# Adaptive modulation by running sums over features, and the first products tile by tile

## The chip, the cores and the metric

The kernel runs on one core of one Trainium2 chip. The metric is device microseconds (us) from start to end of one execution; lower is better. Engines are named as in the profile: PE is TensorE, DVE is VectorE, ACT is ScalarE, SP issues all transfers.

## The reference

Everything is fp32. A first block of 512 tokens by 1024 features is followed by two more layers, which the change does not touch. What matters here is the modulation and the first product:

```python
mod = jax.nn.silu(c) @ w_ada[layer] + b_ada[layer]          # c: 1 x 1024, w_ada: 1024 x 6144
shift1, scale1, gate1, shift2, scale2, gate2 = [
    m[:, None, :] for m in jnp.split(mod, N_MOD, axis=-1)]
h = rms_norm(x, g_pre_mix[layer]) * (1.0 + scale1) + shift1
proj = h @ w_in[layer]                                      # 1024 x 3584
```

`gate1`, `shift2`, `scale2` and `gate2` are needed later: `gate1` after the output projection, `shift2` and `scale2` ahead of the first MLP product, `gate2` after the MLP.

## The kernel before, in words

**Units.** All matrices reach the core in units of 128 x 1024 fp32, 512 KB each, through a ring of five buffers `RAW`. SP issues unit i when the buffer of unit i-5 was consumed (semaphore `s_taken`, raised by DVE). `unit_list` writes the order by hand: the 16 `ada` units of scale1 and shift1 first (j = 1, then j = 0), then the 28 units of `w_in`, one further `ada` unit behind each of 24 of them, then the rest.

**Products in three terms.** A weight unit is split into two parts that PE takes at full rate: ACT rounds it to `WH` (L1603), DVE subtracts to get `WL` (L904, the function `lo_to`). Activations are split the same way, into `HH` (ACT) and `HL` (DVE). Each tile product is three matmuls of 128 x 512 (L443, L444, L445, the function `three`). The first four `w_in` units are the values: one `group` of 96 matmuls, 12 for each of the 8 feature tiles k. Then each `w_in` unit is one `column` of 24 matmuls: 8 of queries and keys (`qk`), 4 of gates (`g`), 12 of the convolution. `walk` lets ACT and DVE prepare units up to two or three columns ahead of PE; there are four slots of `WH` and `WL`.

**Modulation.** In an `ada` unit the 128 partitions are 128 of the 1024 inputs, the free dimension the 1024 features of one of the six vectors. DVE multiplies it by silu(c), one scalar for each partition, and adds it to an accumulator of 128 x 1024 (L853 for the first, L856 for the next seven). After eight units PE adds up the partitions: for the gates with `ONES` as the stationary operand (L407, one row in every partition), for scales and shifts with eight matmuls of one column (L401, 16 rows in the trace), which leave features in partitions in bank 7. DVE adds the bias into `MOD` (L873) and so frees bank 7.

**The start.** Transfers: `VEC` (94 KB), `CST` (97.5 KB, with the identity matrix and the rotary frequencies), `X` in one piece (2048 KB), five `ada` units (2560 KB), positions (256 KB, one row read into all partitions), then units as buffers come free. ACT squares the tokens (L1689); after seven modulation units DVE computes the norm factors (`token_factors`, L1004 and ten small instructions) and both engines scale the tokens (`normed_tokens`, L1693, L1011). PE transposes them in 32 steps (L602); ACT and DVE copy them to `Z`. When scale1 and shift1 are there, ACT writes `HH` (L1805) and DVE `TMP` (L1149) and `HL` (L1156), and the first product starts. The rotary angles are computed by DVE and ACT between these (from L1109). After each `qk` column DVE rotates it (`rotate`, L1172 to L1176, four instructions).

## Time and profile before

| | |
|---|---|
| median of 3 runs | 1545.19 us (1545.18 to 1547.71) |
| profiled execution, its own time | 1542.9 us |
| its span in the profile | 1541.1 us |
| PE busy | 1474.4 us, 96% |
| DVE busy | 880.6 us, 57% |
| ACT busy | 546.9 us, 35% |
| matmuls | 7232 |
| read from memory | 155.65 MB, 102 GB/s over the span |

The profile is one execution, 1542.9 us long; its span, from the first instruction to the last, is 1.8 us shorter. A busy share is the time in which an engine had an instruction in work. Waits are put down to the engine or transfer whose end released them.

### The profile page before, as it was taken

The numbers are of one execution on the slowest core, as the hardware profiler recorded it, in microseconds if no ns is written. First come the engines' busy times: TensorE is split into PE (matmuls) and PEld (weight loads), VectorE is DVE, ScalarE is ACT, GpSimd is POOL, SyncE is SP. The second block draws the span as 40 slices with busy tenths as digits, with TensorE's granted clock in tenths as the row PEclk, the third lists the DMA queues.
The fourth block names the chain that finished last, engine by engine and source line by source line (L and its number), as shares of the span: only waits on it lengthen the run. The fifth ranks groups of instructions, "written<-read, shape, count | busy, mean of one in ns | idle before, by whom it ended". The sixth has DMA issues, their size and how long they took to land.

```text
span 1541.1 us, 18491 instructions
## 1 busy us (share of the span) xinstructions
PE 1474.4 (96%) x7232; PEld 1221.7 (79%) x7232; DVE 880.6 (57%) x1702; ACT 546.9 (35%) x957; POOL 0.2 (0%) x4
## 2 busy tenths in 40 slices
PE   2899999899999999999999899999999999999897
PEld 2778777788888888798888788888888888888776
DVE  5886646554333333665466434524778777787435
ACT  2412123632223223542232323533345434444331
POOL 0000000000000000000000000000000000000000
PEclk9899999999999999999999999999999999999999
DMA  8745322153222223213232222322222111111111
GB/s 303 272 160 206 121 83 96 56 185 143 96 96 96 96 96 110 82 58 121 100 106 83 96 96 82 110 96 77 74 69 69 69 69 69 64 64 67 68 69 55
DMA packets 43526, 158.94 MB, mean 103 GB/s; under 512 B 4784, under 2 KB 5040, under 8 KB 43312
## 3 DMA queue, kind: packets, MB, share of 16 engines
q1 hardware_dynamic: 43440, 157.76, 29.1%
q8 instruction: 58, 0.95, 0.3%
q14 instruction: 28, 0.23, 0.0%
HBM read 155.65 MB, written 2.10 MB: 102 GB/s over the span
## 4 chain that ended last, share of the span: by engine, by line
PE 89%; DVE 5%; ACT 3%; issue 1%; DMA 1%; SPq 0%; ACTq 0%; DVEq 0%
PE PS L443 27%; PE PS L445 26%; PE PS L444 26%; PE PS L728 1%; DMA RAW<-in_ada 1%; PE PS L776 1%; PE PS L739 1%; DVE Z L856 1%; PE PS L780 1%; PE PS L770 1%; PE PS L748 1%; PE PS L756 1%; PE PS L625 1%; PE PS L634 1%; PE PS L804 1%
## 5 line engine op out<-in xcount | busy, mean ns | idle before, releaser
L443 PE MATMUL PS<-HH,WH 128*128 128x512 f32 (+1 forms) x1152 | 459.8, 399 | 4.3 <-ACT TMP L1705 2.3
L445 PE MATMUL PS<-HH,WL 128*128 128x512 f32 (+1 forms) x1152 | 438.0, 380 | 0.0
L444 PE MATMUL PS<-HL,WH 128*128 128x512 f32 (+1 forms) x1152 | 436.6, 379 | 0.0
L904 DVE TENSOR_TENSOR WL<-RAW,WH 128x1024 fp32r<-128x1024 f32 x226 | 274.8, 1219 | 81.5 <-ACT WH L1603 81.3
L1603 ACT ACTIVATE WH<-RAW 128x1024 fp32r<-128x1024 f32 x226 | 238.1, 1056 | 195.7 <-PE PS L445 168.2
L443 PEld LDWEIGHTS PS<-HH,WH 128*128 128x128 f32 x1152 | 218.5, 190 | 46.0 <-issue 6.3
L445 PEld LDWEIGHTS PS<-HH,WL 128*128 128x128 f32 x1152 | 218.3, 189 | 42.0
L444 PEld LDWEIGHTS PS<-HL,WH 128*128 128x128 f32 x1152 | 218.9, 190 | 40.3 <-issue 3.6
L443 PE MATMUL PS<-WH,ZH 128*128 128x512 f32 x400 | 156.7, 392 | 3.9 <-issue 3.9
L444 PE MATMUL PS<-WL,ZH 128*128 128x512 f32 x400 | 156.6, 391 | 0.0
L445 PE MATMUL PS<-WH,ZL 128*128 128x512 f32 x400 | 156.4, 391 | 0.0
L951 DVE TENSOR_TENSOR ZL<-Z,ZH 128x512 fp32r<-128x512 f32 x52 | 35.5, 690 | 144.4 <-ACT ZH L1660 144.4
L443 PE MATMUL PS<-WH,HH 128*128 128x512 f32 x224 | 90.6, 404 | 7.3 <-DVE Z L1390 3.3
L443 PEld LDWEIGHTS PS<-WH,ZH 128*128 128x128 f32 x400 | 75.7, 189 | 20.1 <-issue 4.3
L445 PE MATMUL PS<-WH,HL 128*128 128x512 f32 x224 | 89.0, 397 | 0.0
L1660 ACT ACTIVATE ZH<-Z 128x512 fp32r<-128x512 f32 x52 | 32.2, 629 | 159.7 <-PE PS L445 159.7
L444 PE MATMUL PS<-WL,HH 128*128 128x512 f32 x224 | 88.8, 396 | 0.0
L445 PEld LDWEIGHTS PS<-WH,ZL 128*128 128x128 f32 x400 | 75.7, 189 | 15.9
L444 PEld LDWEIGHTS PS<-WL,ZH 128*128 128x128 f32 x400 | 75.7, 189 | 15.7
L1270 DVE TENSOR_TENSOR Z<-TMP 128x512 f32<-128x512 f32 x32 | 22.0, 692 | 90.7 <-ACT TMP L1870 90.6
L1870 ACT ACTIVATE TMP<-PS 128x512 f32<-128x512 f32 x32 | 19.0, 597 | 110.1 <-PE PS L445 109.9
L443 PEld LDWEIGHTS PS<-WH,HH 128*128 128x128 f32 x224 | 43.1, 193 | 17.7 <-DVE Z L1390 3.7
(223 smaller groups left out, 1666.8 us busy)
## 6 DMA issues: line engine op xcount, KB each, us to landing
RAW<-in_w_fc SPq DMA_DIRECT2D x64, 512.0 KB, 3.2
RAW<-in_hgrn_in SPq DMA_DIRECT2D x64, 512.0 KB, 3.2
RAW<-in_ada SPq DMA_DIRECT2D x48, 512.0 KB, 3.7
RAW<-in_pool_in SPq DMA_DIRECT2D x40, 512.0 KB, 3.2
RAW<-in_w_in SPq DMA_DIRECT2D x28, 512.0 KB, 4.5
RAW<-in_pool_out SPq DMA_DIRECT2D x16, 512.0 KB, 3.2
RAW<-in_hgrn_out SPq DMA_DIRECT2D x16, 512.0 KB, 3.2
RAW<-in_w_out SPq DMA_DIRECT2D x8, 512.0 KB, 3.2
```

The lines of the kernel that those rows point to most:

```text
L443: e.matmul(out, wh, xh, start=first, stop=False)
L444: e.matmul(out, wh, xl, start=False, stop=False)
L445: return e.matmul(out, wl, xh, start=False, stop=last)
L625: e.matmul(PS[b][:, 0:n], Z[:, 12 + h, 128 * i:128 * i + 128], Z[:, 8 + h, 128 * i:T], start=True, stop=True).then_inc(banks.full[b], bank ...
L634: m = e.matmul(PS[ob][:, 128 * i:T], VT[:, i, 128 * h:128 * h + 128], RETA[:, RETO[i]:RETO[i] + n], start=i == 0, stop=i == 3)
L728: m = e.matmul(PAIR[:, 256 * i:256 * i + 192], t.f[:, c], t.qp[:, i, :], start=True, stop=True)
L904: e.tensor_tensor(lo, RAW[:, i % NR, :], hi.bitcast(F32), ALU.subtract).then_inc(taken.sem, taken(i))
L951: e.tensor_tensor(lo, Z[:, k, :], hi.bitcast(F32), ALU.subtract).then_inc(zlo.sem, zlo(z))
L1270: e.tensor_tensor(Z[:, f, :], TMP[:, f % 2, :], TMP[:, f % 2, :], ALU.mult).then_inc(zdone.sem, zdone("fc1", f))
L1603: e.activation(place(s)[0], RAW[:, i % NR, :], ACT.Copy).then_inc(whi.sem, whi(s))
L1660: e.activation(z_place(z)[0], Z[:, k, :], ACT.Copy).then_inc(zhi.sem, zhi(z))
L1870: e.activation(TMP[:, f % 2, :], PS[f if f < 4 else f % 7][:, :], ACT.Relu).then_inc(banks.free[f if f < 4 else f % 7], 1)
```

## The change

`shift1`, `scale1`, `shift2` and `scale2` are computed with the features in the partitions. Their `ada` units are stored transposed: 128 features by the 1024 inputs. DVE multiplies such a unit by a row of silu(c), held in all partitions as `CB`, and the same instruction adds up its products along the free dimension (`accum_out`) into one column of `MOD`. So one unit gives 128 finished values and needs no PE. The gates keep the old way.

The order of units changes with it. The first 20 are four times: one `w_in` unit, then scale and shift of feature tile f, then of tile f+1. The four `w_in` units of the first group thus come between. The token tiles are transposed into banks 4 to 7, the first four ahead of the group and the others after its first four tiles. ACT reads a tile from its bank with scale and shift (new L1791), then rounds it to `HH` (L1794), DVE forms `HL` (`first_low`, new L1130), and PE multiplies tile k as soon as `HL` of tile k is there. Rotary angles now stand ahead of the norm factors on DVE. `c` is loaded as a row into all partitions (512 KB); `CST` is loaded behind the first five units; `X` comes in four pieces; the masks are loaded as bytes (128 KB for 512 KB) and DVE's cast of them goes. Behind `w_in` 12, 13 and 14 stand two `ada` units in place of one.

```diff
 def unit_list():
 
 
-    out = [("ada", 8 * j + k, False) for j in (1, 0) for k in range(8)]
+    out = []
+    for f in range(8):
+        if f % 2 == 0:
+            out.append(("w_in", f // 2, True))
+        out += [("ada", 2 * f, False), ("ada", 2 * f + 1, False)]
     ada = iter(range(16, 48))
-    for n in range(28):
+    for n in range(4, 28):
         out.append(("w_in", n, True))
-        if 1 <= n <= 24:
-            out.append(("ada", next(ada), False))
+        if n <= 24:
+            out += [("ada", next(ada), False) for _ in range(2 if 12 <= n < 15 else 1)]
     for name, n in (("w_out", 8), ("w_fc1", 32), ("w_fc2", 32), ("pool_in", 40), ("pool_out", 16),
                     ("hgrn_in", 64), ("hgrn_out", 16)):
         for i in range(n):
...
-            e.dma_start(CST[:, :], a["cst"][:, 0:C_D]).then_inc(s_cst, 16)
-            e.dma_start(X[:, :, :], a["x"].rearrange("(i p) d -> p i d", p=128)).then_inc(s_x, 16)
+            e.dma_start(flat(0), a["rows"][5].partition_broadcast(128)).then_inc(s_c, 16)
+            e.dma_start(POSI, a["positions"].partition_broadcast(128)).then_inc(s_pos, 16)
+            for t in range(4):
+                e.dma_start(X[:, t, :], a["x"][128 * t:128 * t + 128, :]).then_inc(s_x[t], 16)
             for i in range(NR):
                 load(i)
...
                 j, k = divmod(UNITS[i][1], 8)
-                if k < 7:
+                if j not in (2, 5) or k < 7:
                     return
                 e.wait_ge(taken.sem, taken.of(i))
-                if j in (2, 5):
-                    gate_row(j, 0, 7)
-                    if j == 2:
-                        gate_row(j, 1, 3)
-                    return
-                claim(7)
-                for c in range(8):
-                    m = e.matmul(PS[7][:, 16 + c:17 + c], ACCS[1 if j == 1 else 0][:, 128 * c:128 * c + 128],
-                                 ONES[:, 0:1], start=True, stop=True)
-                m.then_inc(banks.full[7], banks.fill(("ada", j), 7))
+                gate_row(j, 0, 7)
+                if j == 2:
+                    gate_row(j, 1, 3)
...
+            def first_tokens(f):
+                b = 4 + f % 4
+                claim(b)
+                for t in range(4):
+                    m = e.transpose(PS[b][:, 128 * t:128 * t + 128], normal("x", t)[:, 128 * f:128 * f + 128],
+                                    IDN)
+                m.then_inc(banks.full[b], banks.fill(("x", "t", f), b))
+
-            run(group([("v", j) for j in range(4)], [0, 1, 2, 3], True, "in"))
+            e.wait_ge(s_cst, 16)
+            e.wait_ge(normed.sem, normed.of("x", 2))
+            e.wait_ge(own.sem, own.of("normed", "x", 3))
+            for f in range(4):
+                first_tokens(f)
+            for k, _ in enumerate(group([("v", j) for j in range(4)], [0, 1, 2, 3], True, "in")):
+                if k < 4:
+                    first_tokens(4 + k)
...
                 j, k = divmod(UNITS[i][1], 8)
-                src, sc, acc = RAW[:, i % NR, :], COL[:, k:k + 1], ACCS[1 if j == 1 else 0]
+                src = RAW[:, i % NR, :]
                 e.wait_ge(*landed(i))
-                if k == 0:
-                    if j > 1:
-                        e.wait_ge(*banks.made(("ada", 2, 1) if j == 3 else ("ada", j - 1 if j > 2 else 0)))
-                    e.tensor_scalar(acc, src, sc, None, ALU.mult).then_inc(taken.sem, taken(i))
+                if j == 3 and k == 0:
+                    e.wait_ge(*banks.made(("ada", 2, 1)))
+                if j in (3, 4) or k:
+                    e.wait_ge(taken.sem, p.acc)
+                if j in (3, 4):
+                    e.scalar_tensor_tensor(out=ACC, in0=src, scalar=1.0, in1=CB[:, :], op0=ALU.mult,
+                                           op1=ALU.mult, accum_out=MOD[:, 8 * j + k:8 * j + k + 1]).then_inc(
+                                               taken.sem, taken(i))
+                elif k == 0:
+                    e.tensor_scalar(ACC, src, COL[:, k:k + 1], None, ALU.mult).then_inc(taken.sem, taken(i))
                 else:
-                    e.wait_ge(taken.sem, p.acc)
...
 
+            def first_modulation(f):
+
+                for j in (1, 0):
+                    i = UNITS.index(("ada", 2 * f + 1 - j, False))
+                    e.wait_ge(*landed(i))
+                    if f:
+                        e.wait_ge(taken.sem, taken.of(UNITS.index(("ada", 2 * f - 1 - j, False))))
+                    c = 8 if j else 16
+                    e.scalar_tensor_tensor(out=flat(6 if j else 4), in0=RAW[:, i % NR, :], scalar=1.0,
+                                           in1=CB[:, :], op0=ALU.mult, op1=ALU.mult,
+                                           accum_out=MOD[:, c + f:c + f + 1]).then_inc(taken.sem, taken(i))
...
+            e.wait_ge(s_c, 16)
+            e.wait_ge(copied.sem, copied.of("silu row"))
+            e.tensor_tensor(CB[:, :], flat(2), flat(0), ALU.mult).then_inc(own.sem, own("cb"))
+            e.wait_ge(s_pos, 16)
+            e.wait_ge(s_cst, 16)
+            e.tensor_copy(TN, POSI).then_inc(own.sem, own())
...
+                e.scalar_tensor_tensor(out=ANG, in0=TN, scalar=-part, in1=ANG, op0=ALU.mult,
+                                       op1=ALU.add).then_inc(own.sem, own())
+            token_factors("x", 0, 4)
+            normed_tokens("x", 3)
+
+            def first_low(k):
+                e.wait_ge(hhi.sem, hhi.of("in", k))
+                e.tensor_tensor(HL[:, k, :], TMP[:, 2 + k % 2, :], HH[:, k, :].bitcast(F32),
+                                ALU.subtract).then_inc(hlo.sem, hlo("in", k))
+
+            p.next, p.hi, p.unit = 20, 4, 4
+            for f in range(8):
+                if f % 2 == 0:
+                    lo_to(f // 2 + 1)
+                first_modulation(f)
+                if f:
+                    first_low(f - 1)
+                if f == 1:
+                    e.scalar_tensor_tensor(out=TN, in0=ANG, scalar=-1.0, in1=ANG, op0=ALU.mult,
+                                           op1=ALU.max).then_inc(own.sem, own("angle"))
+            first_low(7)
+            lo_to(5)
+            e.wait_ge(copied.sem, copied.of("cos"))
+            e.tensor_tensor(TN, SIN, SIN, ALU.mult).then_inc(own.sem, own())
+            e.scalar_tensor_tensor(out=SIN, in0=SIN, scalar=CST[:, C_SGN:C_SGN + 1], in1=COS,
+                                   op0=ALU.mult, op1=ALU.mult).then_inc(own.sem, own())
+            lo_to(6)
+            e.wait_ge(own.sem, own.n)
+            e.tensor_scalar(COS, TN, -2.0, 1.0, ALU.mult, ALU.add).then_inc(own.sem, own("rot"))
...
+            e.wait_ge(s_c, 16)
+            e.activation(flat(2), flat(0), ACT.Sigmoid).then_inc(copied.sem, copied("silu row"))
...
-            normed_tokens("x", 0)
-            normed_tokens("x", 1)
-            for f in range(0, 8, 2):
+            for t in range(3):
+                normed_tokens("x", t)
+            e.wait_ge(own.sem, own.of("gb"))
+            for f in range(8):
+                b = 4 + f % 4
+                if f % 2 == 0:
+                    hi_to(f // 2 + 1)
+                e.wait_ge(taken.sem, taken.of(UNITS.index(("ada", 2 * f, False))))
+                e.activation(GA[:, f:f + 1], MOD[:, 8 + f:9 + f], ACT.Identity,
+                             scale=VEC[:, V_GPRE1 + f:V_GPRE1 + f + 1], bias=GB[:, f:f + 1]).then_inc(
+                                 copied.sem, copied())
+                e.wait_ge(taken.sem, taken.of(UNITS.index(("ada", 2 * f + 1, False))))
+                e.activation(MOD[:, f:f + 1], MOD[:, 16 + f:17 + f], ACT.Identity,
+                             bias=VEC[:, V_BADA + f:V_BADA + f + 1]).then_inc(copied.sem, copied())
+                if f > 1:
+                    e.wait_ge(hlo.sem, hlo.of("in", f - 2))
                 e.wait_ge(*banks.made(("x", "t", f)))
...
+                e.wait_ge(copied.sem, copied.n)
+                e.activation(TMP[:, 2 + f % 2, :], PS[b][:, :], ACT.Identity, scale=GA[:, f:f + 1],
+                             bias=MOD[:, f:f + 1]).then_inc(banks.free[b], 1)
+                e.wait_ge(*banks.taken(("x", "t", f)))
+                e.activation(HH[:, f, :], TMP[:, 2 + f % 2, :], ACT.Copy).then_inc(hhi.sem, hhi("in", f))
+                if f == 2:
+                    e.wait_ge(own.sem, own.of("angle"))
+                    e.activation(SIN, ANG, ACT.Sin, scale=0.5)
+                    e.activation(COS, TN, ACT.Sin, scale=-0.5, bias=CST[:, C_HPI:C_HPI + 1]).then_inc(
+                        copied.sem, copied("cos"))
+            hi_to(6)
```

How the order of instructions moves, at two places. On DVE ahead of the first product, before (units 0 and 1 are scale1's; `s_raw` is a landed unit, `s_square` the last square of ACT):

```order
L1090 TENSOR_TENSOR COL<-COL,VEC 128x8 [waits s_copied]
L853 TENSOR_SCALAR Z<-RAW,COL 128x1024 [waits s_raw0,s_dve]
L856 SCALAR_TENSOR_TENSOR Z<-RAW,COL,Z 128x1024 [waits s_taken,s_raw1]
...
L856 SCALAR_TENSOR_TENSOR Z<-RAW,COL,Z 128x1024 [waits s_taken,s_raw1]
L1004 TENSOR_SCALAR NW<-SSA 128x4 [waits s_square]
```

and now, at the same place (`s_cst` is the landing of `CST`):

```order
L1110 TENSOR_TENSOR CB<-Z 128x1024 [waits s_copied,s_c]
L1113 CAST TMP<-Z 128x512 [waits s_cst,s_pos]
L1115 TENSOR_SCALAR Z<-TMP,CST 128x512 [waits s_dve]
L1117 TENSOR_SCALAR TMP<-Z 128x512 [waits s_dve]
L1120 TENSOR_SCALAR TMP<-TMP 128x512 [waits s_dve]
L1123 SCALAR_TENSOR_TENSOR Z<-TMP,Z 128x512 [waits s_dve] x4
L1023 TENSOR_SCALAR NW<-SSA 128x4 [waits s_square]
```

The norm factors stood behind seven modulation units and now stand behind the angles, which wait for `CST`. On DVE in the first group now, feature tiles 4 and 5 (L923 is `WL`, L879 a running sum, L1130 `HL`):

```order
L923 TENSOR_TENSOR WL<-RAW,WH 128x1024 [waits s_whi]
L879 SCALAR_TENSOR_TENSOR Z,MOD<-RAW,CB 128x1024 [waits s_taken,s_raw1]
L879 SCALAR_TENSOR_TENSOR Z,MOD<-RAW,CB 128x1024 [waits s_taken,s_raw2]
L1130 TENSOR_TENSOR HL<-TMP,HH 128x512 [waits s_hhi]
L879 SCALAR_TENSOR_TENSOR Z,MOD<-RAW,CB 128x1024 [waits s_taken,s_raw3]
L879 SCALAR_TENSOR_TENSOR Z,MOD<-RAW,CB 128x1024 [waits s_taken,s_raw4]
L1130 TENSOR_TENSOR HL<-TMP,HH 128x512 [waits s_hhi]
```

and on ACT from the same pair of tiles on (L1781 and L1785 give scale and shift of one tile, L1594 is `WH`):

```order
L1594 ACTIVATE WH<-RAW 128x1024 [waits s_raw0]
L1781 ACTIVATE COL<-MOD,COL,VEC 128x1 [waits s_taken]
L1785 ACTIVATE MOD<-MOD,VEC 128x1 [waits s_taken]
L1791 ACTIVATE TMP<-PS,MOD,COL 128x512 [waits s_copied,s_full4,s_hlo]
L1794 ACTIVATE HH<-TMP 128x512 [waits s_free4]
L1781 ACTIVATE COL<-MOD,COL,VEC 128x1 [waits s_taken]
L1785 ACTIVATE MOD<-MOD,VEC 128x1 [waits s_taken]
L1791 ACTIVATE TMP<-PS,MOD,COL 128x512 [waits s_copied,s_full5,s_hlo]
L1794 ACTIVATE HH<-TMP 128x512 [waits s_free5]
L1594 ACTIVATE WH<-RAW 128x1024 [waits s_raw0]
```

Before, the 16 running sums were done ahead of this group; now DVE's next `WL` waits for ACT's `WH`, which stands behind `HH` of an odd tile, which waits for that tile's sums on DVE.

## Rows read from the trace of the kernel before

**Rows 1.** The page, busy time, share of the span and instructions of each engine.

```profile
PE 1474.4 (96%) x7232; PEld 1221.7 (79%) x7232; DVE 880.6 (57%) x1702; ACT 546.9 (35%) x957; POOL 0.2 (0%) x4
```

**Rows 2.** Timeline, the start: start us, length us, engine, line, operation; in brackets idle, releaser.

```profile
11.10 0.75 DVE L853 TENSOR_SCALAR Z<-RAW,COL 128x1024 f32<-128x1024 f32 x1 [7.99 <-DMA RAW<-in_ada]
...
18.60 2.67 DVE L856 SCALAR_TENSOR_TENSOR Z<-RAW,COL,Z 128x1024 f32<-128x1024 f32 x2 [0.85 <-DMA RAW<-in_ada]
...
21.19 0.16 DVE L1004 TENSOR_SCALAR NW<-SSA 128x4 f32<-128x4 f32 x1
...
22.96 2.19 ACT L1693 ACTIVATE Z<-X,COL 128x1024 f32<-128x1024 f32 x2 [8.54 <-DVE COL L997]
```

**Rows 3.** Transfers: instruction, count, size, median us from issue to landing.

```profile
RAW<-in_w_fc SPq DMA_DIRECT2D x64, 512.0 KB, 3.2
...
G<-in_rows SPq DMA_DIRECT2D x1, 512.0 KB, 4.6
```

**Rows 4.** Timeline, DVE before and in the first group, among them the angles.

```profile
37.26 4.05 DVE L856 SCALAR_TENSOR_TENSOR Z<-RAW,COL,Z 128x1024 f32<-128x1024 f32 x3
...
41.23 0.42 DVE L1109 CAST TMP<-Z 128x512 f32<-128x512 int32 x1
...
44.46 1.22 DVE L904 TENSOR_TENSOR WL<-RAW,WH 128x1024 fp32r<-128x1024 f32 x1
...
59.15 1.41 DVE L1121 SCALAR_TENSOR_TENSOR Z<-TMP,Z 128x512 f32<-128x512 f32 x2
```

**Rows 5.** Page, ACT, costliest groups: rounding a weight unit, reading a bank.

```profile
L1603 ACT ACTIVATE WH<-RAW 128x1024 fp32r<-128x1024 f32 x226 | 238.1, 1056 | 195.7 <-PE PS L445 168.2
...
L1870 ACT ACTIVATE TMP<-PS 128x512 f32<-128x512 f32 x32 | 19.0, 597 | 110.1 <-PE PS L445 109.9
```

**Rows 6.** Timeline, ACT in the first group: sine table and cosine.

```profile
58.14 1.28 ACT L1792 ACT_TABLE_LOAD   x1
...
63.52 0.73 ACT L1795 ACTIVATE Z<-TMP,CST 128x512 f32<-128x512 f32 x1 [2.30 <-DVE TMP L1125]
```

**Rows 7.** Timeline, PE: the first product and the first column.

```profile
47.50 0.76 PE L443 MATMUL PS<-WH,HH 128*128 128x512 f32 x1 [2.56 <-issue]
...
50.57 0.40 PE L444 MATMUL PS<-WL,HH 128*128 128x512 f32 x1
...
70.75 0.39 PE L443 MATMUL PS<-HH,WH 128*128 128x512 f32 x1
```

**Rows 8.** Timeline, PE after a pause ahead of the first MLP product.

```profile
285.72 0.36 PE L443 MATMUL PS<-HH,WH 128*128 128x256 f32 x1 [2.35 <-ACT TMP L1705]
```

**Rows 9.** Windows, that stretch: PE, PEld, DVE, ACT, POOL busy, clock, transfer share, GB/s.

```profile
286.00:291.00 5.00, 5.00 (x30) 4.91 (x29) 3.54 (x7) 4.91 (x12) 0.00 (x0) 0.66 0.32 108
```

**Rows 10.** Timeline, PE: gate row, sums over partitions, and the norm sums of the retention.

```profile
85.91 1.98 PE L407 MATMUL PS<-Z,ONES 128*128 128x512 f32 x4 [1.39 <-DVE Z L856]
...
131.32 1.95 PE L401 MATMUL PS<-ONES,Z 128*128 128x1 f32 x16
...
193.03 1.84 PE L401 MATMUL PS<-ONES,Z 128*128 128x1 f32 x16
...
211.31 1.02 PE L580 MATMUL PS<-ONES,TMP 128*128 128x1 f32 x8 [1.64 <-DVE MOD L873]
```

**Rows 11.** Timeline, DVE in the columns of queries and keys.

```profile
96.11 0.69 DVE L1172 TENSOR_TENSOR TMP<-PS,Z 64x512 f32<-64x512 f32 x1 [0.82 <-PE PS L445]
...
98.85 1.28 DVE L856 SCALAR_TENSOR_TENSOR Z<-RAW,COL,Z 128x1024 f32<-128x1024 f32 x1
100.05 1.22 DVE L904 TENSOR_TENSOR WL<-RAW,WH 128x1024 fp32r<-128x1024 f32 x1
101.56 0.69 DVE L1172 TENSOR_TENSOR TMP<-PS,Z 64x512 f32<-64x512 f32 x1 [0.29 <-PE PS L445]
...
105.49 0.68 DVE L882 TENSOR_TENSOR G<-PS,Z 128x512 f32<-128x512 f32 x1
...
108.14 1.22 DVE L904 TENSOR_TENSOR WL<-RAW,WH 128x1024 fp32r<-128x1024 f32 x1
```

More of the change, by code:

```diff
@@ L209, in build @@
             pass
+        with nc.sbuf_tensor("CB", [128, 1024], F32) as CB:
+            pass
         QP = [sb(f"QP{i}", [128, 4, 192]) for i in range(2)]
@@ L1079, in diagonal @@
                 p.spread = name
-            def gains(dst, j, g, one):
-                e.wait_ge(*banks.taken(("ada", j)))
-                e.scalar_tensor_tensor(out=COL[:, dst:dst + 8], in0=MOD[:, 8 * j:8 * j + 8],
-                                       scalar=1.0 if one else 0.0, in1=VEC[:, g:g + 8], op0=ALU.add,
-                                       op1=ALU.mult).then_inc(own.sem, own())
             e.memset(ONES[:, :], 1.0).then_inc(own.sem, own("ones"))
+            e.wait_ge(s_vec, 16)
@@ L1160, in vector_program @@
-            run(group(), turns)
-            run(turns)
-            e.wait_ge(s_msk, 16)
-            e.tensor_copy(MSK[:, :], flat(14)).then_inc(own.sem, own("masks"))
+            e.scalar_tensor_tensor(out=GB, in0=VEC[:, V_BADA + 8:V_BADA + 16], scalar=1.0,
+                                   in1=VEC[:, V_GPRE1:V_GPRE1 + 8], op0=ALU.add, op1=ALU.mult).then_inc(
+                                       own.sem, own("gb"))
+            e.wait_ge(s_c, 16)
+            e.wait_ge(copied.sem, copied.of("silu row"))
@@ L1799, in scalar_program @@
-            turns = angles()
-            next(turns)
-            walk(1)
-            e.wait_ge(*banks.taken(("ada", 0)))
-            for k in range(8):
-                e.wait_ge(*banks.taken(("x", "t", k)))
-                e.activation(HH[:, k, :], Z[:, k, :], ACT.Identity, scale=GA[:, k:k + 1],
-                             bias=MOD[:, k:k + 1]).then_inc(hhi.sem, hhi("in", k))
-                if k in (1, 4):
-                    walk(1 + k // 4)
+            for t in range(3):
+                normed_tokens("x", t)
@@ L1813, in values @@
                 e.activation(VT[:, j, :], PS[j][:, :], ACT.Copy).then_inc(banks.free[j], 1)
-            run(group(values), turns)
-            run(turns)
+            for j in range(4):
+                values(j)
             nb = 0
```

148 lines of the change are left out of this document (36 added, 112 removed).

## The prediction

> **What bounds the kernel now.** First the page: PE is busy for 96% of the span, DVE and ACT are far from it [rows 1]. So only three things can move the time: work that PE no longer does, a wait of PE that goes or comes, and the start, in which PE has nothing to multiply. Then the timeline of the start. The first product begins at 47.50 us and the first column at 70.75 us [rows 7]. Seven matmuls up to 50.57 us run at the low clock level, one in 0.44 us; the other 89 of the group take 20.2 us, 0.227 us each, without a pause. Up to 47.5 us DVE sets the pace with its 16 modulation units, 1.35 us each where one waits for the last [rows 4]. The change attacks this start, so what counts is when the first column can begin. Last, the columns: 5.45 us each (24 by 0.227), in which DVE rotates for 2.74 us and spends 1.20 us on a modulation unit and about 1.2 us on a `WL`, so it has next to nothing in reserve there [rows 11].
>
> **The change, part one: until the group can start.** The norm factors now wait for the angles on DVE, and these for `CST`. Ahead of and with `CST` stand 94 + 512 + 256 + 2048 + 2560 + 97.5 = 5567.5 KB. That is exactly what stood up to the sixth `ada` unit before, which landed at 18.6 us; the first, behind 2751.5 KB, had landed at 11.1 us, so 376 KB/us flow [rows 2]. New among the bytes is the row of `c`, read into all partitions. Such a load took 4.6 us from issue to landing where others of 512 KB took 3.2 us [rows 3]. I add 0.5 us, between nothing and 1.4 us: `CST` lands at 19.1 us. By the section on queues, rings and completion order of the Trainium skill, "DMA: Bandwidth & Descriptors", each engine consumes its descriptors in ring order but completions need not come in the order of issue; if that let the small `CST` pass the units ahead of it, the second rival below would hold. The angles: cast to second product of the range reduction 3.23 us (41.23 to 44.46), two more products 1.41 us [rows 4], so DVE is free at 23.75 us. Factors 1.77 us (21.19 to 22.96) to 25.5 us; ACT scales three tiles, 1.5 times 2.19 us, to 28.8 us [rows 2], and rounds the first `w_in` unit, 1.06 us [rows 5]: at **29.9 us** DVE starts the first `WL`. All five units landed by then, and DVE will be slower (below) than five units in 6.8 us at the rate above, so transfers hide.
>
> **Part two: the group, paced by DVE and ACT in turn.** A running sum reads two fp32 inputs as the old instruction, 1.20 us in sequence [rows 11], and adds up as well. The trace has no such instruction on DVE. If the read of the sum overlaps, it is free; the smallest instructions of DVE take 0.16 us [rows 2], and a full one behind a drained pipe could cost a few tenths. I take 0.1 us, nearest to the small instruction with overlap: 1.30 us, with 0 and 0.3 us as ends. The Trainium skill, "VectorE: DVE Perf Modes", section "Two Vector instructions with no wait between them", says that an op that writes its accumulator is two instructions; it gives no time, and by it the free end would be excluded. Two tiles cost DVE one `WL` 1.2, four sums 5.2 and one `HL` 0.6 us, 7.0 together; the other `HL` fits into what follows. Then DVE waits: ACT needs 0.2 us for the shift, 0.6 us for the bank and 0.6 us for `HH`, 0.2 us of handing over, and 1.05 us for `WH` [rows 5], 2.65 us in all. So a pair takes 9.65 us. The first pair lacks an `HL`: 9.05 us. In the second ACT also does the table load (1.28) and two sines (0.73 each) [rows 6]; counted from the end of the sums of tile 2 at 3.8 us, 1.6 + 2.75 + 0.4 + 1.3 + 1.05 us follow: 10.9 us. The third takes 9.65 us. In the fourth `HL` of tile 6 is ready at 7.6 us. Sum: 9.05 + 10.9 + 9.65 + 7.6 = 37.2 us. PE needs 2.7 us for each of the last two tiles at full clock, which gives 42.6 us. Tile 4 ends near 30.7 us on this scale and `HL` of tile 5 is ready at 34.0 us, so PE pauses for 3.3 us. After a pause of 2.35 us elsewhere PE ran at a granted mean of 0.66 for 5 us [rows 8, 9], thus for 3.4 us at 1.2 GHz, losing 1.7 us of work. Tile 6 follows tile 5 after a pause of 0.5 us that absorbs part, and the low level may begin inside the pause: I add 0.9 us. The column starts at 29.9 + 43.5 = **73.4 us, 2.65 us later than before**. Behind it DVE has about 8.5 us of its own work (three `WL`, three sums, three rotary steps) and 15 us until the third column needs it: hidden.
>
> **Part three: PE's sums over partitions.** Ahead of the group they stood beside DVE's work and are worth nothing by themselves. In the columns two sets of L401 go, 1.95 and 1.84 us [rows 10], with PE otherwise busy on both sides: **3.7 us less**. DVE's bias addition into `MOD` held bank 7, and PE waited for it 1.64 us ahead of the retention's norm sums [rows 10]. This wait goes; PE's next matmuls are columns for which DVE had reserve: **1.6 us less**, with 0 as the other end, should DVE be late there anyway.
>
> **Part four: two modulation units in one column.** From the end of the `qk` column whose sums close gate1, DVE owes by the `WL` of the third gate column: three rotations 8.2, six sums 8.4, the gate row's four instructions 2.65 (105.49 to 108.14), three `WL` 3.6 us, 22.9 us. PE runs four columns meanwhile, 21.8 us [rows 11]. **1.1 us more**, as a wait of PE ahead of that column; 0 to 2.5 us with the price of a sum. Before, the same place held three units fewer.
>
> **At no cost.** The gate row itself, 1.39 us of waiting and 2 us of matmuls, moves three columns back unchanged [rows 10]. The masks' cast and 384 KB go, both hidden beside PE's columns. The silu row, `CB` and `GB` are done while `CST` is in flight.
>
> **Sum.** +2.65 − 3.7 − 1.6 + 1.1 = −1.55 us. The profiled execution took 1542.9 us, so its like would take 1541.35 us; the median is 2.3 us above it, and I move the median by the same: **1543.6 us**. A difference of 0.2%, 3.1 us, is about what a measurement here tells from none.
>
> **The rivals.**
> - *The sum comes free* (chance 0.27). A running sum takes 1.20 us, as its two inputs alone do [rows 11]. 16 in the group give 1.6 us and six in part four 0.6 us; with the clock kept in the pause 0.9 us more: −4.65 us, 1540.5 us.
> - *`CST` passes the units* (0.05). It lands near 12 us and the angles end before the squares. The start moves up by 5 to 6 us, until running sums wait for their units: some 1538 us. Against it: the flow in order of issue [rows 2].
> - *The running sum is dear* (0.17). This is the case of the other sign. At 0.4 us above my price, 22 sums on the path cost 8.8 us: −1.55 + 8.8 = +7.2 us, 1552.4 us. It decides the sign at 0.07 us above my price, and a slowdown beyond 0.2% from 0.21 us, a running sum of 1.51 us.
> - *The clock falls in each pause and bank 7 gives nothing* (0.08). If the level falls at tile 5 and stays low into tile 6, the group ends up to 2.2 us later; without the 1.6 us: +2.25 us, 1547.4 us. The Trainium skill, "TensorE: Matmul & The Clock Gate", section on oscillation, tells of bursts shorter than the waits between them that start slow each time. Here the trace agrees after its pause [rows 8, 9]; early tiles have time to spare in any case, only the last three count.
>
> **The numbers.** The forecast has 0.43; its own range, with 0.05 us either way on a sum and 0.8 us on the clock, is 1541.5 to 1546.5 us. Faster by over 0.2% (under 1542.1 us) are the first two rivals: 0.32. Slower by over 0.2% (over 1548.3 us) is the third, with some of the fourth and of what I have not seen: 0.20. The rest, 0.48, is within. The range that leaves out two in ten is 1539.5 to 1549.5 us.
>
> **What would show it.** The first `WL` of the changed kernel near 29.9 us, the cast of the angles near 19 us. Running sums of 1.30 us in sequence. DVE idle for ACT's `WH` three times, 2 to 3.5 us. First product near 37 us, first column near 73.4 us, the low clock once late in the group. No L401, no wait ahead of the retention's sums, about 1 us ahead of the third gate column. I am wrong if the cast comes much sooner, or if a running sum is off by 0.1 us, or if PE stands still in the columns for longer than here.

## The result, and the profile after

The changed kernel took 1538.51 us (median of 4 runs, 1536.32 to 1539.49), the kernel before 1546.45 us (median of 4 beside it, 1545.18 to 1548.03): ratio 0.9946, 95% interval 0.9929 to 0.9963, or 7.9 us less. Copies of both, run later, gave 1538.24 us (5 runs) and 1544.41 us (11 runs), the ratio of the changed one 0.9959 (0.9946 to 0.9973), 6.3 us less. The forecast was 1543.6 us; its range ended at 1539.5 us, about 1 us above the result. The profiled execution took 1538.69 us with a span of 1536.9 us, 4.2 us less than the profiled span of before.

The page of the changed kernel, engines' busy time, share and instructions; PE lost 64 instructions, two sets of 16 in the columns and two ahead of the group:

```profile
PE 1467.9 (96%) x7168; PEld 1212.9 (79%) x7168; DVE 874.4 (57%) x1719; ACT 557.2 (36%) x979; POOL 0.2 (0%) x4
```

Timeline of DVE in the changed kernel: start us, length us, engine, line, operation, and in brackets idle time and releaser.

```profile
19.78 0.43 DVE L1113 CAST TMP<-Z 128x512 f32<-128x512 int32 x1 [11.27 <-DMA CST<-in_cst]
...
30.45 1.23 DVE L923 TENSOR_TENSOR WL<-RAW,WH 128x1024 fp32r<-128x1024 f32 x1 [3.45 <-ACT WH L1594]
31.60 1.22 DVE L879 SCALAR_TENSOR_TENSOR Z<-RAW,CB 128x1024 f32<-128x1024 f32 x1
32.74 0.08 DVE L879 DVE_READ_ACCUMULATOR Z<-RAW,CB 128x1 f32 x1
32.74 1.22 DVE L879 SCALAR_TENSOR_TENSOR Z<-RAW,CB 128x1024 f32<-128x1024 f32 x1
33.89 0.08 DVE L879 DVE_READ_ACCUMULATOR Z<-RAW,CB 128x1 f32 x1
...
39.10 1.23 DVE L923 TENSOR_TENSOR WL<-RAW,WH 128x1024 fp32r<-128x1024 f32 x1 [1.64 <-ACT WH L1594]
...
50.06 1.23 DVE L923 TENSOR_TENSOR WL<-RAW,WH 128x1024 fp32r<-128x1024 f32 x1 [3.95 <-ACT WH L1594]
...
59.34 1.22 DVE L923 TENSOR_TENSOR WL<-RAW,WH 128x1024 fp32r<-128x1024 f32 x1 [2.26 <-ACT WH L1594]
```

The first `WL` starts at 30.45 us, 0.55 us behind the forecast, because the cast, which waits for `CST`, starts at 19.78 us and not at 19.1 us. The starts of two running sums, 31.60 and 32.74 us, lie 1.14 us apart (1.145 us on average over two steps), not 1.30 us. The read of the accumulator is a row of its own of 0.08 us, and it starts at the same moment as the next sum: it costs nothing in sequence. The four starts of `WL` are the beats of the group: 8.65, 10.96 and 9.28 us between them, where the prediction had 9.05, 10.9 and 9.65 us.

Timeline of ACT in the changed kernel, the turn of tile 0, and `WH` at the end of tile 1:

```profile
32.86 0.39 ACT L1781 ACTIVATE COL<-MOD,COL,VEC 128x1 f32<-128x1 f32 x1 [2.44 <-DVE Z L879]
34.00 0.29 ACT L1785 ACTIVATE MOD<-MOD,VEC 128x1 f32<-128x1 f32 x1 [0.76 <-DVE Z L879]
34.39 0.78 ACT L1791 ACTIVATE TMP<-PS,MOD,COL 128x512 f32<-128x512 f32 x1
35.20 0.63 ACT L1794 ACTIVATE HH<-TMP 128x512 fp32r<-128x512 f32 x1
...
38.03 1.04 ACT L1594 ACTIVATE WH<-RAW 128x1024 fp32r<-128x1024 f32 x1
```

The prediction had 0.2 us for the shift and 0.6 us for the bank; the rows say 0.29 (0.39 from start to start) and 0.78 us. These small steps stand on the path in each turn too and took back part of what the sums gave.

Timeline of PE in the changed kernel, which answers to [rows 7, 8, 10]:

```profile
37.01 0.76 PE L445 MATMUL PS<-WH,HH 128*128 128x512 f32 x1 [3.87 <-DVE HL L1130]
54.24 0.79 PE L445 MATMUL PS<-WH,HH 128*128 128x512 f32 x1 [4.31 <-DVE HL L1130]
63.51 0.50 PE L445 MATMUL PS<-WH,HH 128*128 128x512 f32 x1 [0.37 <-DVE HL L1130]
...
72.03 0.39 PE L445 MATMUL PS<-HH,WH 128*128 128x512 f32 x1
...
103.50 1.98 PE L409 MATMUL PS<-Z,ONES 128*128 128x512 f32 x4 [1.39 <-DVE Z L863]
130.16 0.50 PE L445 MATMUL PS<-HH,WH 128*128 128x512 f32 x1 [0.18 <-DVE WL L923]
207.50 0.95 PE L582 MATMUL PS<-ONES,TMP 128*128 128x1 f32 x8
```

A window of the group (busy time and count of PE, PEld, DVE, ACT, POOL, then granted clock, transfer share, GB/s):

```profile
54.00:60.00 6.00, 5.76 (x15) 4.50 (x16) 3.74 (x7) 4.34 (x7) 0.00 (x0) 0.50 0.97 321
```

PE pauses for 4.31 us ahead of tile 3 (54.24 us) and runs at the low level behind it, so tiles 3 and 4 take so long that ahead of tile 5 (63.51 us) it pauses for only 0.37 us.

The first column starts 1.28 us later than in [rows 7], not 2.65 us. The gate row waits its 1.39 us as before. Ahead of the third gate column PE waits 0.18 us, not 1.1 us. The sums over partitions are gone, and ahead of the retention's norm sums (207.50 us, against 211.31 us in [rows 10]) there is no wait. At that row the kernel is 3.81 us ahead, and that is nearly all of the 4.2 us that the two spans differ by; the rest arises near 880 us (numbers 1 and 2).

### The profile page after: what moved, and what is told of

It is laid out like the page before. It is cut to its first block, busy times and chain, and to the rows that moved or that the text cites. A ratio compares the mean times of both kernels' runs of the same rounds, so it can differ in the third digit from the quotient of the medians.

```text
span 1536.9 us, 18402 instructions
## 1 busy us (share of the span) xinstructions
PE 1467.9 (96%) x7168; PEld 1212.9 (79%) x7168; DVE 874.4 (57%) x1719; ACT 557.2 (36%) x979; POOL 0.2 (0%) x4
## 4 chain that ended last, share of the span: by engine, by line
PE 86%; DVE 6%; ACT 4%; issue 2%; DMA 1%; SPq 0%; ACTq 0%; DVEq 0%
PE PS L445 26%; PE PS L447 26%; PE PS L446 26%; PE PS L729 1%; PE PS L777 1%; PE PS L740 1%; DMA CST<-in_cst 1%; ACT WH L1594 1%; PE PS L781 1%; PE PS L771 1%; DVE WL L923 1%; PE PS L749 1%; PE PS L757 1%; DVE Z L879 1%; PE PS L626 1%
## 5 line engine op out<-in xcount | busy, mean ns | idle before, releaser
L923 DVE TENSOR_TENSOR WL<-RAW,WH 128x1024 fp32r<-128x1024 f32 x226 | 275.0, 1219 | 92.5 <-ACT WH L1594 92.2
L1594 ACT ACTIVATE WH<-RAW 128x1024 fp32r<-128x1024 f32 x226 | 238.1, 1056 | 195.2 <-PE PS L447 145.0
L1863 ACT ACTIVATE TMP<-PS 128x512 f32<-128x512 f32 x32 | 19.1, 600 | 110.1 <-PE PS L447 109.8
```

The lines of the kernel that those rows point to most:

```text
L923: e.tensor_tensor(lo, RAW[:, i % NR, :], hi.bitcast(F32), ALU.subtract).then_inc(taken.sem, taken(i))
L1594: e.activation(place(s)[0], RAW[:, i % NR, :], ACT.Copy).then_inc(whi.sem, whi(s))
L1863: e.activation(TMP[:, f % 2, :], PS[f if f < 4 else f % 7][:, :], ACT.Relu).then_inc(banks.free[f if f < 4 else f % 7], 1)
```

## The experiments

Each kernel ran beside the kernel before on one chip; the runs of before had medians of 1544.9 to 1545.0 us in all three sets. Unless said otherwise, an edit is made to the changed kernel, whose copy (the same kernel, run again) took 1538.24 us.

**1, 2. The two kernels again.** No edit.

Expected of the copy of before: 

> The kernel before once more, timed against itself, with a second profile. The profiled execution of before (1542.9 us) lies 2.3 to 5.1 us under its four timed ones, while the changed kernel's profiled one (1538.69 us) lies among its own. Theory A, the two profiles differ by 4.2 us and that is the true effect; the rest of the measured 8 us is scatter of before: this run's times spread from 1543 to 1548 us, and so does the ratio. Theory B, before really takes 1546 us and its profile was a lucky execution: all times lie at 1545 us and above, and the new profile shows some 3 us more of low clock or of waiting somewhere.

Expected of the copy of the changed kernel: 

> The changed kernel once more, to have it on the same chip as the others and with five rounds. By theory A (scatter of before) 4 to 5 us below before; by theory B 7 to 8 us below it. The profile shows the first column at 72 us and running sums of 1.15 us again.

Measured: 1544.41 us (1542.56 to 1548.14, 11 runs) and 1538.24 us (1537.05 to 1539.31, 5 runs). So the execution of before on which the sum was built, 1542.9 us, lies at the low end of that kernel's executions, while that of the changed kernel (1538.69 us) lies in the middle of its own. The times of before scatter as theory A had it, and the difference of 6.2 us lies between the 4 to 5 us of A and the 7 to 8 us of B: neither is decided. In the copy of the changed kernel the first column starts at 71.07 us, and its cast comes at 18.80 us in place of 19.78 us. Each run also gives its mean granted clock: on average 0.9861 over 15 runs of before and 0.9894 over the 5 of the copy. The two profiled executions had 0.987 both.

One difference that no edit touches shows in all four profiles. PE pauses for 3.9 us in each, and resumes at 878.88 us in the copy of before and at 873.83 us in the copy of the changed kernel. Windows of 10 us from there on, in this order:

```profile
878.88:888.88 10.00, 10.00 (x34) 8.04 (x35) 4.60 (x6) 2.71 (x4) 0.00 (x0) 0.75 0.35 107
```

```profile
873.83:883.83 10.00, 10.00 (x37) 8.09 (x38) 5.20 (x6) 2.72 (x4) 0.00 (x0) 0.83 0.32 105
```

The low level around this resumption lasts 6.8 us in both profiles of before and 3.4 us in both of the changed kernel (by windows of 0.5 us), and from the resumption to the next transposes by L439 (L441 now), at 966.57 and 960.85 us, the copies take 87.7 and 87.0 us. So the longer low stretch costs 0.6 to 0.7 us. It does not mark the kernel before: of the profiles below, those of numbers 3, 5, 7, 9, 10 and 12 have the long stretch and those of 4, 6, 8 and 11 the short one. What decides between the two stays open.

**3. `CST` ahead of the units.**

```
             e.dma_start(VEC[:, :], a["vec"]).then_inc(s_vec, 16)
+            e.dma_start(CST[:, :], a["cst"][:, 0:C_D]).then_inc(s_cst, 16)
...
             for i in range(NR):
                 load(i)
-            e.dma_start(CST[:, :], a["cst"][:, 0:C_D]).then_inc(s_cst, 16)
```

Expected: 

> One part is changed: CST is loaded right behind VEC in place of behind five units. Theory C, the start is set by the landing of CST: angles then run ahead of the squares, the norm factors start at the end of the squares near 14.3 us in place of 24.5 us, the first WL near 20.5 us in place of 30.45 us, and the kernel gets 9 to 10 us faster than the changed kernel. Rival: units of the matrix then arrive too late for DVE, it waits for RAW in the group, and the gain is 4 us or less.

Measured: 1528.74 us (ratio to before 0.9896, 0.9882 to 0.9909), 9.5 us less than the copy of the changed kernel. DVE of this kernel:

```profile
7.99 0.43 DVE L1113 CAST TMP<-Z 128x512 f32<-128x512 int32 x1 [0.44 <-DMA Z<-in_positions]
...
20.23 1.23 DVE L923 TENSOR_TENSOR WL<-RAW,WH 128x1024 fp32r<-128x1024 f32 x1 [3.45 <-ACT WH L1594]
```

The first `WL` starts 10.22 us earlier than in the changed kernel, and the end moves with it: the theory held. So the wait for `CST` is the start's bound, as part one had it, and no transfer of a unit takes its place.

**4. ACT rounds a weight unit ahead of the odd tile.**

```
                 if f % 2 == 0:
                     hi_to(f // 2 + 1)
+                elif f < 7:
+                    hi_to(f // 2 + 2)
```

Expected: 

> One part is changed: ACT rounds the next w_in unit ahead of the odd tile of a pair in place of behind it. Theory D, DVE's three waits for WH (1.6, 4.0 and 2.3 us) are pauses of the whole group: the group ends 7 us earlier. Rival: the pauses hide another limit, the transfers (five units need 6.8 us, DVE's work for two tiles 7.0 us) or PE at the low clock, and the gain is 4 us or less.

Measured: 1532.85 us (0.9922, 0.9909 to 0.9934), 5.4 us less, between the theory's 7 us and the rival's 4 us. The timeline of DVE shows the four `WL` at 30.31, 37.24, 46.18 and 53.11 us; the second and the fourth wait for nothing, the third 1.93 us. A pair without a wait takes 6.93 us: one `WL`, four sums and two `HL`. The first column starts at 66.71 us, 5.3 us earlier. This shows the alternation of part two: ACT's rounding stood in the turn, and a pair was DVE's work plus that of ACT. Some of the rival is there too, for in the last pair DVE waits 0.84 us for a transfer, which it never does in the changed kernel's group:

```profile
59.20 1.23 DVE L879 SCALAR_TENSOR_TENSOR Z<-RAW,CB 128x1024 f32<-128x1024 f32 x1 [0.84 <-DMA RAW<-in_ada]
```

**5. Eight more products in the group.**

```
                     c = 8 if j else 16
+                    if j:
+                        e.tensor_tensor(ACC, RAW[:, i % NR, :], CB[:, :], ALU.mult)
                     e.scalar_tensor_tensor(out=flat(6 if j else 4), ...
```

The products are read by nobody. Expected: 

> A measurement of how much of a running sum lies on the path of the group: each of the eight tiles gets one more product of two fp32 inputs on VectorE (unit times row, into ACC), ahead of its first running sum, that nobody reads. Theory: DVE and ACT take turns and every sum of the group delays ACT, so all eight count in full: 8 x 1.2 = 9.6 us above the changed kernel. Rival: ACT sets the pace, and DVE, which stands idle for some 9 us in all for ACT's roundings, takes the work in those gaps: 2 to 4 us above it, with those idle times shorter by as much.

Measured: 1547.64 us (1544.44 to 1549.81, 10 runs), 9.4 us more; expected 9.6 us. The first column starts at 80.07 us instead of 72.03 us, 8.0 us later. DVE's idle time ahead of each `WL` is hardly changed: 1.64, 2.81 and 2.26 us, and only the second is shorter, by 1.14 us. From first `WL` (30.33 us) to first column the trace has 8.2 us more. The products take 1.14 us each in sequence, 9.1 us in all, so 0.9 us of them is missing, which is about that shorter wait. The theory held; that 9.4 us came so near to 9.6 us is partly chance, as the trace shows 8.2 us in the group. So an instruction of DVE in the group counts nearly in full (where ACT does not have the sines to do), and the price of a running sum multiplies by 14 to 16.

**6. The factor 1.0 from SBUF.**

```
-                    e.scalar_tensor_tensor(..., in0=RAW[:, i % NR, :], scalar=1.0,
+                    e.scalar_tensor_tensor(..., in0=RAW[:, i % NR, :], scalar=ONES[:, 0:1].bitcast(F32),
```

The same in the columns' running sums. Expected: 

> The running sums take their factor 1.0 from a column of ones in SBUF in place of a constant in the instruction; all 32 of them. The old products with a column as factor took 1.20 us in sequence, the running sums 1.15 us. Theory: the operand in SBUF is what costs the 0.05 us, so the running sums take 1.20 us in sequence and the group ends 16 x 0.05 = 0.8 us later, 1 us in all. Rival: the difference comes from the old form's second operand, which DVE itself had just written, and the running sums stay at 1.15 us: no difference.

Measured: 1540.05 us (1538.57 to 1542.82, 9 runs), 1.8 us more than the copy, and 0.9976 of before (0.9966 to 0.9985). The intervals of the two kernels overlap, but the trace is plain. DVE of this kernel:

```profile
30.64 1.28 DVE L879 SCALAR_TENSOR_TENSOR Z<-RAW,ONES,CB 128x1024 f32<-128x1024 f32 x1
31.84 0.08 DVE L879 DVE_READ_ACCUMULATOR Z<-RAW,ONES,CB 128x1 f32 x1
31.84 1.28 DVE L879 SCALAR_TENSOR_TENSOR Z<-RAW,ONES,CB 128x1024 f32<-128x1024 f32 x1
```

1.28 us each and 1.20 us in sequence: exactly the old instruction of [rows 11]. The theory held: the operand from SBUF costs 0.06 us of an instruction's duration, and adding up costs nothing. From first `WL` (29.49 us) to first column (71.90 us) the group takes 42.41 us against 41.58 us, 0.83 us or 16 x 0.05.

**7. Part three undone.** The group keeps its running sums; scale2 and shift2 are summed by PE:

```
-                if j in (3, 4):
-                    e.scalar_tensor_tensor(out=ACC, in0=src, scalar=1.0, in1=CB[:, :], op0=ALU.mult,
-                                           op1=ALU.mult, accum_out=MOD[...])
...
+                claim(7)
+                for c in range(8):
+                    m = e.matmul(PS[7][:, 16 + c:17 + c], ACC[:, 128 * c:128 * c + 128],
+                                 ONES[:, 0:1], start=True, stop=True)
```

Expected: 

> Only the group's modulation keeps the running sums; scale2 and shift2 are again products on VectorE that TensorE adds up over the partitions (two sets of eight one-column matmuls in bank 7). Theory, as in the prediction's part three: 3.7 us for the two sets and 1.6 us for the wait ahead of the retention's norm sums come back, so 5.3 us above the changed kernel. Rival: the wait for bank 7 gives nothing, 3.7 us above it, and the trace shows DVE late at another place, or PE waiting in the retention by as much as the sums would have saved.

Measured: 1553.5 us (1550.85 to 1556.44, 5 runs), 15.3 us more, three times what both theories gave. The timeline of PE shows where:

```profile
135.87 3.58 PE L410 MATMUL PS<-ONES,Z 128*128 128x1 f32 x16 [3.69 <-DVE Z L866]
...
202.07 1.84 PE L410 MATMUL PS<-ONES,Z 128*128 128x1 f32 x16
...
220.35 1.02 PE L589 MATMUL PS<-ONES,TMP 128*128 128x1 f32 x8 [1.64 <-DVE MOD L895]
```

PE waits 3.69 us for DVE and the sums behind the wait run at the low level, 3.58 us in place of 1.9 us. That level lasts 10.2 us (by windows of 0.5 us from 135 us on), which costs PE an estimated 4.7 us. The wait for bank 7 is there again, at 1.64 us as before. From first column to the last norm sums the trace has 13.6 us more than the changed kernel's (71.24 to 220.35 us against 72.03 to 207.50 us): 3.7 us for the two sets, 5.3 us for the two waits, 4.7 us for the low level. That DVE was late there through the doubled units was the guess. This raised the question of the doubled units, for the next two.

**8. Part four undone.** One modulation unit behind each `w_in` unit up to the 28th:

```
-        if n <= 24:
-            out += [("ada", next(ada), False) for _ in range(2 if 12 <= n < 15 else 1)]
+        out.append(("ada", next(ada), False))
```

Expected: 

> Part four alone is undone: one modulation unit behind each w_in unit up to the 28th, none doubled. By the trace of the changed kernel PE waits only 0.18 us ahead of the third gate column, so the theory is that the doubled units cost next to nothing: 0.2 us less than the changed kernel, which these runs can't tell from none, and that wait is gone from the trace. Rival, the prediction's part four: 1.1 us less.

Measured: 1537.39 us (1535.71 to 1539.56, 5 runs), 0.85 us less, which these runs can't tell from none; the wait of 0.18 us is gone from the trace.

**9. Parts three and four undone** (both edits). Expected: 

> scale2 and shift2 summed by TensorE again, and one modulation unit per column. With the doubled units this undoing cost 15.3 us in place of the 5.3 us of the prediction's part three. Theory: the doubled units put DVE 4 us behind, TensorE asks for the sums in the order of the units and waits for that backlog, twice, and drops to the low clock after it; with one unit per column there is no backlog, the two sets cost their own 3.7 us and the wait for bank 7 1.6 us: 5.3 us above e_single, some 1543.5 us. Rival: the backlog comes from the later start of the columns' modulation in all (four units behind, not three), so it stays: 10 us or more above e_single.

Measured: 1550.09 us (1548.06 to 1551.73, 5 runs), 12.7 us above number 8. So the doubled units explain only 2.6 of the 10 us that were too many in number 7. The theory fell. The rival had the size, but not the place: PE does not wait for DVE at the first set. The timeline of PE:

```profile
152.34 1.84 PE L409 MATMUL PS<-ONES,Z 128*128 128x1 f32 x16
...
160.37 1.83 PE L588 MATMUL PS<-ONES,TMP 128*128 128x1 f32 x8 [3.11 <-DVE MOD L894]
162.07 0.77 PE L451 MATMUL PS<-HH,WH 128*128 128x512 f32 x1
162.64 0.63 PE L452 MATMUL PS<-HL,WH 128*128 128x512 f32 x1
...
222.15 1.95 PE L409 MATMUL PS<-ONES,Z 128*128 128x1 f32 x16 [0.30 <-DVE Z L865]
```

and its windows around both places (clock third from the right):

```profile
158.00:170.00 12.00, 9.63 (x29) 7.26 (x30) 5.07 (x9) 0.41 (x1) 0.00 (x0) 0.72 0.00 1
216.00:230.00 14.00, 13.70 (x60) 10.73 (x59) 8.25 (x21) 2.61 (x4) 0.00 (x0) 0.88 0.44 150
```

In number 8 the clock is 1.00 in both windows. Here PE waits 3.11 us for the addition of the bias, which DVE's program reaches only at 160.07 us, behind the retention's own steps, and then runs at the low level. From these norm sums to the next the trace has 20.3 us, where number 8 has 17.0 us: the low level behind the wait costs 3.3 us more, on top of the wait. Behind the second set it lasts 3.4 us, an estimated 1.7 us of work. Together, 3.8 us for the sets, 3.4 us for the two waits and 5.0 us for the low level are 12.2 us. By the row at which PE waits for `DG` (242.58 us, against 231.01 us in number 8) the trace has fallen back by 12.3 us, counted from the first column (71.24 and 71.96 us); the medians differ by 12.7 us.

**10. Numbers 3 and 4 together.** Expected: 

> CST is loaded right behind VEC, and ACT rounds the next w_in unit ahead of the odd tile; nothing else differs from the changed kernel. Theory: the two act in different places, the one moves the whole group up, the other takes ACT's rounding out of the turn between DVE and ACT, so the gains found for each alone add: 9.5 + 5.4 = 14.9 us less than the changed kernel, some 1523.5 us. Rival 1: with both, DVE asks for five units in less than the 6.8 us that the transfers take for them and waits for landings; then the gain of the second shrinks to about 2 us, 1527 us, and the trace shows waits of DVE for RAW out of the DMA queue in the group. Rival 2: PE pauses more often at the faster pace and loses clock, 1525 to 1527 us, with no wait of DVE for transfers.

Measured: 1522.16 us (0.9862, 0.9848 to 0.9875), 16.1 us less than the changed kernel where the parts add to 14.9 us; the medians do not tell the two apart. The theory held. Windows of the group in this kernel, and in the changed one over the stretch that answers to it:

```profile
20.00:60.00 40.00, 34.53 (x146) 27.67 (x145) 36.40 (x54) 27.55 (x46) 0.00 (x0) 1.00 0.87 308
```

```profile
30.00:70.00 40.00, 31.41 (x120) 24.80 (x119) 30.13 (x47) 24.00 (x41) 0.00 (x0) 0.83 0.77 262
```

DVE is busy for 36.4 of 40 us and waits for no landing in the group. PE still pauses for 3.63 us ahead of its first product and later for 1.12 and 0.71 us, but the clock stays at its high level. Both rivals were wrong.

**11. The first unit rounded ahead of the tokens**, on top of number 10:

```
+            hi_to(1)
             for t in range(3):
                 normed_tokens("x", t)
```

Expected: 

> e_both, and ACT rounds the first w_in unit ahead of scaling the first three token tiles, not behind them. In e_both DVE waits 3.45 us for that rounding. Theory: DVE starts its first WL about 3.3 us sooner and keeps that lead down the group, since every later turn is set by DVE's sums; only ACT's scaled tokens come 1 us later, which the transposes can stand: 2.5 to 3.3 us less than e_both, 1519.3 us. Rival: ACT sets the next turns, as it takes up tile 0 only after its tokens and three transposes, and DVE's lead turns into a wait for the second WH: 0 to 1 us less.

Measured: 1517.68 us (1517.64 to 1520.56, 5 runs), 0.9832 of before (0.9818 to 0.9846): the fastest here, 4.5 us below number 10. The wait of 3.45 us ahead of the first `WL` is 0.34 us; the first column starts at 52.50 us against 55.49 us. Those 3 us are shown. A further 0.7 us comes from the pause of numbers 1 and 2, behind which number 10 has the long low stretch and number 11 the short one; the last 0.8 us lie within what the medians leave open.

**12. The sines behind tile 6**, on top of number 11:

```
-                if f == 2:
+                if f == 6:
                     e.wait_ge(own.sem, own.of("angle"))
                     e.activation(SIN, ANG, ACT.Sin, scale=0.5)
```

Expected: 

> e_first, and the two sines and their table load move from behind tile 2 to behind tile 6. In e_both DVE waits 1.92 us for the WH behind the sines. Theory: that wait shrinks by the 2.7 us that the sines hold ACT, so it goes; behind tile 6 ACT has tile 7 and two roundings ahead of it and the sines put these back by 2.7 us, which the last WL can't stand fully: 0 to 1.9 us less than e_first. Rival: the group's end is set by HL of tile 7, which ACT now reaches 2.7 us later, so it is 1 us or more slower than e_first.

Measured: 1521.73 us (1520.23 to 1522.91, 4 runs), 4.0 us more. The rival had the sign, but not the place. DVE:

```profile
38.91 1.23 DVE L923 TENSOR_TENSOR WL<-RAW,WH 128x1024 fp32r<-128x1024 f32 x1 [1.05 <-ACT WH L1594]
...
48.93 0.69 DVE L1130 TENSOR_TENSOR HL<-TMP,HH 128x512 fp32r<-128x512 f32 x1 [3.00 <-ACT HH L1797]
...
62.91 1.29 DVE L863 SCALAR_TENSOR_TENSOR Z<-RAW,COL,Z 128x1024 f32<-128x1024 f32 x1 [1.81 <-DMA RAW<-in_ada]
```

`HL` of tile 7 waits 3.00 us (1.31 us in number 11), and the first column begins at 52.57 us, no later. But DVE is 0.8 us later at its last `WL` of the group and frees its buffers that much later, the transfers into them are issued 0.8 us later, and at 62.91 us it waits 1.81 us for a landing (0.44 us in number 11), 1.4 us behind number 11. PE pays at the gate row, waiting 2.35 us for DVE instead of 1.39 us.

That is 1.0 us of the 3.3 us by which the two profiled executions differ. The rest lies in stretches that the edit does not touch. PE waits for ACT ahead of transposes at 277.05 us (275.99 us in number 11). Windows behind it, in number 12 and then in number 11:

```profile
277.00:283.00 6.00, 5.95 (x38) 5.98 (x39) 1.95 (x5) 5.03 (x13) 0.00 (x0) 0.72 0.00 0
```

```profile
276.00:282.00 6.00, 6.00 (x52) 6.00 (x53) 2.21 (x6) 5.34 (x14) 0.00 (x0) 1.00 0.00 0
```

From there to the next transposes by that line, at 621.54 and 618.86 us, number 12 takes 1.6 us longer. Near 856 us it has the long low stretch, 0.7 us. So the move is shown to cost 1.0 us in the columns. Whether the two low stretches follow from it or vary from run to run stays open.

## Why the prediction was wrong

The mechanism held in all four parts: the start waits for `CST`, DVE and ACT take turns, the sums of PE and the wait go, and PE waits ahead of the third gate column. What failed are three sizes: the price of a running sum, the place and cost of the low clock in the group, and the step from the profiled execution to the median.

**Part one held.** The cast came at 19.8 us, where the landing of `CST` was forecast for 19.1 us; the first `WL` stood 0.55 us behind the forecast. In the copy the cast came at 18.80 us, so the landing itself scatters by 1 us from run to run.

**Part two failed at the price of the running sum**: "I take 0.1 us, nearest to the small instruction with overlap: 1.30 us". It measured 1.15 us, below even the free end of 1.20 us, because the constant factor saves what the accumulation was feared to cost (number 6). Number 5 shows that such an error counts nearly in full. Two of the 16 sums stand beside ACT's sines and count for nothing, so this term alone was 14 x 0.155 = 2.2 us too high in the group.

The 0.9 us for the clock failed by its place. The prediction had a pause of 3.3 us ahead of tile 5 with the low level behind it. The trace has the pause of 4.31 us ahead of tile 3, with the low level there. Tiles 3 and 4 had time to spare for it, and PE paused for 0.37 us ahead of tile 5. The last three tiles ran from 63.51 to 72.03 us in 8.5 us, against 36 x 0.227 = 8.2 us at full clock.

Against it went the 0.55 us of the start, ACT's steps in three turns, 0.27, 0.43 and 0.30 us too low (from the last sum to `WH`; the bank and the shift too low, the sines too high), and the 0.3 us of the last three tiles. Small differences of `WL` and `HL` take back 0.1 us. Together, −2.2 − 0.9 + 0.55 + 1.0 + 0.3 − 0.1 = −1.35 us; the column came 1.37 us before the forecast.

The clause "by it the free end would be excluded" went wrong with it. The Trainium skill's "VectorE: DVE Perf Modes", section "Two Vector instructions with no wait between them", is right that there are two instructions, and the trace agrees: it has the second row. But that row of 0.08 us lies under the next sum, so two instructions are not two costs here.

**Part three held in size.** 3.8 us for the two sets and 1.64 us for the wait were gone. Numbers 7 and 9 show more: in the new order of units the same PE sums would have cost 12.7 to 15.3 us, since the additions and products that they wait for sit later in DVE's program and the low clock comes with the waits (5.0 us of it in number 9). Taking one part back measures it in its new surroundings, not the share that it had in the change.

**Part four failed by the same price, and by a slip.** 1.1 us was forecast, 0.18 us measured. The prediction put the six sums at 8.4 us, 1.40 us each, where its own price of 1.30 us gives 7.8 us; that alone would have made 0.5 us of the 1.1 us. In the trace of DVE the six take 7.25 us, 1.21 us each, since the second of two in a row starts 1.34 us after the first. Number 8 agrees with the small wait.

**The sum, mended.** −1.55 − 1.37 − 0.92 = −3.84 us, and the trace is 3.81 us ahead at the retention's norm sums. This is "the sum comes free", the first rival, to which the prediction gave 0.27: its price and nearly its size (−4.65 us), though it too moved the result to 1540.5 us only.

**The anchor failed too**, the step from the profiled execution to the median: "the median is 2.3 us above it, and I move the median by the same". Even with −3.84 us this gives 1541.4 us, and 1538.5 us was measured. The medians of before lie 1.5 to 3.6 us above its profiled execution (1544.4 to 1546.5 us against 1542.9 us), those of the changed kernel 0.2 and 0.5 us below its own. So of the 5.1 us between forecast and result 2.3 us are errors of the sum, 2.5 us the anchor, and the remaining 0.3 us arise behind the norm sums, mostly by the shorter low stretch near 880 us.

Why a usual execution of before takes longer than its profiled one stays open. The mean clocks of the runs, 0.9861 and 0.9894, point to more of the low level in before, but a mean clock is not a time. The changed kernel's profile has 41.8 us at the low level in all and its copy 31.8 us, yet the two differ by 1.1 us, of which 1.0 us is there at the first column already, from the earlier cast. 6.8 of these 10 us lay at the first tiles of the group, which have time to spare. Of the kept profiles of before, the copy has 3.4 us more of the low level, at its start (0.69 over 30:52 us in place of 0.77), and its first column comes 0.3 us later.

## What to carry to other kernels

Where two engines take turns, first find out which instructions stand in the turn: there an error of 0.1 us in the price of one is multiplied by their number, and a bound from both sides must also ask what else differs in the instruction, such as where its scalar comes from. What helped far more than the change was to take something out of the turn: a small transfer loaded first (9.5 us) and a rounding done one tile sooner (5.4 us). And a wait of an engine late in one place is priced together with all that is ordered behind it: the same sums over partitions were worth 5.4 us in one order of units and 12.7 to 15.3 us in another.

## What the runs showed that was not expected

- A sum with accumulator over 128x1024 fp32 takes 1.22 us (1.15 us in sequence) with a constant factor and 1.28 us (1.20 us in sequence) with a factor in SBUF; the read of the accumulator, 0.08 us, overlaps the next instruction.
- The low clock after a wait costs more than the wait's row shows: in number 9, behind 3.11 us of waiting and eight matmuls of one column (1.83 us at the low level, 0.95 us else), a window of 12 us had a mean clock of 0.72, and the stretch took 3.3 us longer on top of the wait. In number 10 PE paused up to 3.6 us in the group and the clock stayed at 1.00.
- The same pause of 3.9 us near 880 us goes with 3.4 us at the low level in some profiles and 6.8 us in others, with no edit near it; the longer one costs 0.6 to 0.7 us. A window at a fixed time would have shown a clock of 0.81 against 1.00 there, mostly because the program had moved by 5 us: windows are compared from the same instruction on.
